# Expert loop of a one-core hybrid SSD/gMLP/MoE step: gate/up of block b, down of block b-1, then the turning of block b's gated rows

## Chip, core and metric

The kernel runs on one core of a Trainium2 chip. The metric is device time in microseconds (us), the median of three runs. All numbers of the profile come from one profiled execution. Engines are PE (matrix multiplication; PEld are its weight loads), DVE (VectorE), ACT (ScalarE), POOL (GpSimd) and SP (the queue of plain transfers). Each engine runs its own instruction stream in program order and meets the others through semaphores. Its sequencer reads that stream; in the rows PEldq, DVEq, ACTq and POOLq are instructions which a sequencer carries out itself.

## What is computed

One step of an encoder layer over 4096 prompt rows and 128 sample rows (33 tiles of 128 rows, 1024 columns, float32): mixing layers first, then a mixture of experts and a last norm. The change touches only the mixture. Each row goes to 2 of 32 experts; its 8448 (row, expert) slots are sorted by expert and padded to blocks of 128 slots:

```
def run_block(args):
    toks, e = args
    xb = h_pad[toks]
    return (jax.nn.silu(xb @ w_gate[e]) * (xb @ w_up[e])) @ w_down[e]
...
ys = ys.reshape(n_slots, -1) * slot_w[:, None].astype(ys.dtype)
out = jnp.zeros((T + 1, ys.shape[1]), ys.dtype).at[slot_tok].add(ys)[:T]
```

`xb` is 128 x 1024, gate and up are 1024 x 256 each, down is 256 x 1024. The number of blocks depends on the data: at least 66, at most 98, and 80 in this execution (block numbers 0 to 79; the count is rounded up to pairs).

## The kernel before

Phase 1 (the mixing layers, 33 tiles) is left as it is. Phase 2 is a loop over expert blocks, unrolled in pairs by `over_pairs`: 33 pairs always run (`SURE`), and each later pair stands in an `If` on a register. Every engine has its own `step(b)`; the order of the calls within it is written by hand and is the order of work.

For block b the chain is: POOL gathers 128 rows (`gather`); ACT copies three quarters of them into other buffers (`move`, 12 copies, L1733) and DVE transposes them in pieces (`turn`, L1778 to L1782) into `hT`; PE multiplies with gate and up (`pe_gate_up`, L1659, 8 matmuls, each float32 matmul two records in the trace); ACT takes the SiLU of the gate half (`silu`, L1741); DVE multiplies it by the up half (`gate`, L1789) and raises `hb_ready`; PE turns the product (`pe_hidden`, L1669); ACT copies it out (`hidden`, L1746) and raises `hbT_out`; PE multiplies with down (`pe_down`, L1678, 4 matmuls) and raises `dn_full`; DVE scales and adds the residual (`weigh`, L1799); POOL stores that as the first result (`keep`, L1560) or the second is added to the first (`earlier`, L1555, and `add_first`, L1807); ACT sums squares (`squares`, L1750), POOL makes the root (`root_of`, L1588 and L1590, raising `fin_r`), DVE applies the last norm (`norm`, L1793, which waits for `fin_r`) and POOL stores (`store`).

POOL's order in `step(b)` is keep(b-1), residual(b+1), gather(b+5), root_of for block b-2, earlier(b), store(b-2). PE's `step(b)` begins with three reads of a table into registers (`pe_weights` and `entry`, L1415: where the weights of a block lie, and how many loads must have landed). Before the change the steps were

```
PE:  gate/up(b+1) k 0..3, hidden(b), gate/up(b+1) k 4..7, down(b)
DVE: weigh(b-1), turn(b+2), gate(b+1), norm, add_first(b-1)
ACT: hidden(b), squares, move(b+3) 0..5, silu(b+1), move(b+3) 6..11
```

and the last PE step also computed a gate/up product of a block that is not there. After the loop DVE, ACT and POOL each read the last block's number from memory into a register (`last_n`, L1833 on DVE); then DVE weighs, adds and norms what is left of the last two blocks, and POOL stores them.

Of the kernel before, what the change touches and what calls it, by code (L numbers as in the profile page):

```python
# [16 lines left out]
I32 = mybir.dt.int32  # L17
# [4 lines left out]
P = 128  # L22
D = 1024
KD = D // P
# [85 lines left out]
def after(eng, sem, n):  # L110

    if n > 0:
        eng.wait_ge(sem, n)
# [8 lines left out]
def build(nc, x_rows, x_cols, consts_in, cols_in, bcast_in, w_in, w_out, w_out_T_in, ws_in, ws_smp_in, cache_in, st_old_in,  # L122
          st_T_in, slot_in, w_exp, final_g, y_out, conv_prompt, ssm_prompt, conv_sample, ssm_sample, gmlp_v_sample):
    ctx = ExitStack()
    with ctx:
# [1281 lines left out]
        y_buf = [x_res[0][:, :], x_res[1][:, :]]  # L1407
        first_i, last_i = (lng_b[:, k * P:(k + 1) * P].bitcast(I32) for k in range(2))
        final_w = mv[:, 0:1]
        final_i = lng_b[:, 2 * P:2 * P + 2].bitcast(I32)  # L1410
        SURE = 2 * T // P // 2
        PAIRS = NBLK // 2
# [129 lines left out]
        def pool_phase2(pool):  # L1542
# [69 lines left out]
            pool.wait_ge(convp_stored, 16)  # L1612
            pool.wait_ge(spill_set, 16)
            residual(0)
            used = over_pairs(pool, step)

            last_n = (pool.value_load(misc[0:1, 4:5], min_val=2 * SURE - 1, max_val=2 * PAIRS - 1), 2 * used)
            for u in range(2):
                pool.wait_ge(s["fin_sq"], last_n[u])
                nc.gpsimd.tensor_tensor(spare[:, u:u + 1], neg_half[:, 0:1], neg_half[:, 0:1], ALU.mult)  # L1620
# [26 lines left out]
        def pe_gate_up(pe, b, weights, k0, k1):  # L1647

            u = b % 2
            slot, loads = weights  # L1650
            if k0 == 0:
                pe.wait_ge(w_loaded, loads)
                if b < 2:
                    for k in range(2):
                        pe.wait_ge(s[f"gx_out{k}"], b + 1)
                after(pe, s["rows_turned"], b - 1)
                after(pe, s["hb_ready"], b - 1)
            for k in range(k0, k1):
                mm = nc.tensor.matmul(PB[u][:, :], hT[u][:, k, :], arena[:, bass.ds(slot + k * 2 * DE, 2 * DE)],  # L1659
                                      start=k == 0, stop=k == KD - 1)  # L1660
            if k1 == KD:
                mm.then_inc(s["gu_full"], 1)

        def pe_hidden(pe, b):

# [5 lines left out]

        def pe_down(pe, b, slot):

            pe.wait_ge(s["hbT_out"], b + 1)
            for n in range(2):
                after(pe, s["dn_out"], 2 * (b - 2) + n + 1)
                for k in range(2):
                    mm = nc.tensor.matmul(dn_bank[b % 2][n], hTb[:, k, :],  # L1678
                                          arena[:, bass.ds(slot + KD * 2 * DE + k * D + n * 512, 512)], start=k == 0, stop=k == 1)
            mm.then_inc(s["dn_full"], 1)  # L1680
# [17 lines left out]
        def pe_phase2(pe):  # L1698
            pe_table_rows(pe)
            pe.wait_ge(s["tables"], 1)  # L1700
            weights0 = pe_weights(pe, 0)
            pe.wait_ge(s["lists_out"], 2)

            def step(b):
                weights = pe_weights(pe, b + 1)
                slot = entry(pe, TAB_SLOT, b, 0, SLOT_AT[2])
                pe_gate_up(pe, b + 1, weights, 0, 4)
                pe_hidden(pe, b)
                pe_gate_up(pe, b + 1, weights, 4, KD)
                pe_down(pe, b, slot)  # L1710
            pe_rows(pe, 0)
            pe_rows(pe, 1)
            pe_gate_up(pe, 0, weights0, 0, KD)
            pe.wait_ge(s["smp_new"], 8)
            over_pairs(pe, step)

        def act_phase2(act):
            act.wait_ge(x2_stored, 16 * NT)
# [31 lines left out]
                nc.scalar.activation(h2[:, :], src, ACT.Square, accum_out=sq[:, u:u + 1]).then_inc(s["fin_sq"], 1)  # L1750

            def step(b):
                hidden(b)
                if b > 1:
                    squares(b % 2, f_buf[b % 2], b - 1)
                move(b + 3, 0, 6)
                silu(b + 1)
                move(b + 3, 6, 12)
            rows0(0)
            rows0(1)  # L1760
            silu(0)
            move(2, 0, 12)
            used = over_pairs(act, step)
            last_n = (act.value_load(misc[0:1, 4:5], min_val=2 * SURE - 1, max_val=2 * PAIRS - 1), 2 * used)
# [4 lines left out]
        def dve_phase2(dve, st):  # L1769
# [37 lines left out]
                V.tensor_tensor(f_buf[u], y_buf[u], m_buf[u], ALU.add).then_inc(s["first_added"], 1)  # L1807

            def step(b):
                if b > 0:  # L1810
                    dve.wait_ge(s["dn_full"], b + 1)
                    dve.wait_ge(x2_back[1 - b % 2], 16 * ((b + 1) // 2))
                    after(dve, first_kept, 16 * (b - 2))
                    weigh(1 - b % 2, wt[:, b - 1:b])
                turn(b + 2)
                gate(b + 1)
                if b % 2 and b // 2 >= SURE - 1:

                    V.tensor_copy(final_i, last_i[:, b - 1:b + 1])
                    V.tensor_copy(final_w, wt[:, b:b + 1])  # L1820
# [6 lines left out]
            dve.wait_ge(s["tables"], 1)  # L1827
            rows1(0)
            rows1(1)
            gate(0)  # L1830
            dve.wait_ge(gf_loaded, 16)
            used = over_pairs(dve, step)
            last_n = (dve.value_load(misc[0:1, 4:5], min_val=2 * SURE - 1, max_val=2 * PAIRS - 1), 2 * used)  # L1833
# [141 lines left out]
```

## Time and profile before

| | us |
|---|---|
| median of 3 runs (lowest, highest) | 2788.34 (2787.91, 2789.7) |
| the profiled execution's own time | 2790.36 |
| its span, first to last instruction | 2788.5 |
| PE busy, share of the span | 2737.2, 98% |
| DVE busy | 1883.0, 68% |
| ACT busy | 1454.7, 52% |
| POOL busy | 818.0, 29% |
| mean granted clock of PE | 0.991 |

The busy times are over the whole span, phase 1 included. In the rows further down a line gives the start (or the stretch), the duration, the engine and line, what is written and read, and in brackets the idle time before and who ended it.

### The profile page before, as it was taken

What the parts mean: (1) busy time and instruction counts of PE and PEld (TensorE: products, weight loads), DVE (VectorE), ACT (ScalarE), POOL (GpSimd) and SP (SyncE); (2) the same over time, 40 slices, a digit from 0 to 9 for tenths busy, and PEclk for the clock granted to TensorE, in tenths of its full rate; (3) what the DMA queues carried; (4) which work ended last, traced back from release to release, by engine and by line L of the source; (5) the groups of instructions that cost most, each with busy time, mean ns of one, the idle gap of its engine ahead of it and who ended that gap; (6) DMA issues with size and microseconds to landing.
All of it is one profiled execution on the core that took longest, in us unless ns stands there. A gap on an engine that the chain in (4) does not pass through costs nothing.

```text
span 2788.5 us, 38529 instructions
## 1 busy us (share of the span) xinstructions
PE 2737.2 (98%) x11715; PEld 1768.6 (63%) x11715; DVE 1883.0 (68%) x5154; ACT 1454.7 (52%) x3396; POOL 818.0 (29%) x1368
## 2 busy tenths in 40 slices
PE   8999999999999999999999999997999999999997
PEld 6777677767776777677767776763444444444443
DVE  5776767676767676767676767665666666666665
ACT  2445544454455444544454445434666666666665
POOL 1121112111211121112111111112556555556555
PEclk9999999999999999999999999998999999999999
DMA  7311111111111111111111111156888677778864
GB/s 305 136 64 46 69 67 48 46 69 61 54 46 69 64 51 46 69 59 56 46 69 61 54 46 61 42 199 252 307 291 294 236 274 255 280 258 293 317 215 146
DMA packets 104914, 377.91 MB, mean 136 GB/s; under 512 B 32713, under 2 KB 34642, under 8 KB 94706
## 3 DMA queue, kind: packets, MB, share of 16 engines
q1 hardware_dynamic: 44226, 236.13, 23.1%
q0 software_dynamic: 60480, 139.24, 14.8%
q8 instruction: 102, 1.67, 0.2%
q14 instruction: 106, 0.87, 0.1%
HBM read 326.14 MB, written 123.03 MB: 161 GB/s over the span
## 4 chain that ended last, share of the span: by engine, by line
PE 95%; DMA 2%; DVE 1%; ACT 1%; issue 1%; SPq 0%; POOL 0%; POOLq 0%; DVEq 0%; ACTq 0%
PE PB L367 24%; PE PB L1659 20%; PE PB L378 16%; PE PB L457 12%; PE SS L1678 5%; PE TB L1678 5%; PE YB L457 4%; PE YB L411 2%; DMA arena<-in_w_in 1%; PE SS L420 1%; PE SS L424 1%; PE TB L433 1%; PE YB L1669 1%; PE MB L402 1%; PE YB L515 0%
## 5 line engine op out<-in xcount | busy, mean ns | idle before, releaser
L367 PE MATMUL PB<-arena,hT 128*128 128x512 f32 (+2 forms) x2112 | 728.3, 498 | 1.8 <-ACT xT L590 1.1
L1659 PE MATMUL PB<-arena,hT 128*128 x1296 | 582.5, 592 | 0.0
L367 PEld LDWEIGHTS PB<-arena,hT 128*128 128x128 f32 x2112 | 396.7, 190 | 276.9 <-issue 229.7
L378 PE MATMUL PB<-hT,arena 128*128 128x128 f32 x4224 | 487.5, 276 | 4.7 <-DVE arena L1148 4.6
L378 PEld LDWEIGHTS PB<-hT,arena 128*128 128x128 f32 x4224 | 481.8, 193 | 8.9 <-issue 4.9
L1659 PEld LDWEIGHTS PB<-arena,hT 128*128 128x128 f32 x1296 | 239.9, 190 | 271.2 <-issue 271.2
L1185 POOL TENSOR_SCALAR rs<-sq 128x2 f32<-128x2 f32 (+1 forms) x66 | 14.2, 216 | 1254.7 <-ACT h L750 910.3
L457 PE MATMUL PB<-arena,tT 128*128 128x274 f32 (+1 forms) x1056 | 361.6, 497 | 0.3 <-ACT tT L644 0.3
L457 PEld LDWEIGHTS PB<-arena,tT 128*128 128x128 f32 x1056 | 197.1, 192 | 142.7 <-issue 123.4
L636 ACT ACTIVATE yb<-ycat 32x128 f32<-32x128 f32 x768 | 235.9, 307 | 89.3 <-DVE ycat L933 48.7
L1789 DVE TENSOR_TENSOR gv<-ycat,PB 128x256 f32<-128x256 f32 x81 | 34.1, 421 | 290.1 <-ACT ycat L1741 280.8
L823 DVE SCALAR_TENSOR_TENSOR xc<-xT,cols,xc 128x128 f32<-128x128 f32 x792 | 216.8, 347 | 3.5
L750 ACT ACTIVATE h<-x_res 128x1024 f32<-128x1024 f32 x33 | 34.9, 1057 | 336.5 <-DVE x_res L942 336.5
L1746 ACT ACTIVATE xdt<-YB 128x256 f32<-128x256 f32 x80 | 30.6, 383 | 280.9 <-PE YB L1669 270.2
L1678 PE MATMUL TB<-arena,xdt 128*128 x320 | 143.9, 592 | 0.0
L1678 PE MATMUL SS<-arena,xdt 128*128 x320 | 143.8, 592 | 0.0
L590 ACT ACTIVATE xT<-PB 128x512 f32<-128x512 f32 x64 | 38.1, 597 | 188.6 <-PE PB L378 187.8
L1733 ACT ACTIVATE zz<-x_in 32x256 f32<-32x256 f32 x320 | 132.0, 413 | 3.8
L457 PE MATMUL YB<-arena,tT 128*128 128x274 f32 x528 | 127.6, 394 | 0.0
L1560 POOL DMA_INDIRECT out_y<-arena,bc x79 | 89.1, 1128 | 95.4 <-DVE arena L1793 84.9
L821 DVE TENSOR_SCALAR xc<-xT,cols 128x128 f32<-128x128 f32 x264 | 70.8, 344 | 66.0 <-issue 66.0
L1555 POOL DMA_INDIRECT xT<-x_rows,bc x81 | 95.6, 1181 | 64.3 <-DMA x_rows<-x_res,bc 34.4
(292 smaller groups left out, 4109.0 us busy)
## 6 DMA issues: line engine op xcount, KB each, us to landing
arena<-in_w_expert SPq DMA_DIRECT2D x32, 2048.0 KB
arena<-in_w_expert SPq DMA_DIRECT2D x32, 1024.0 KB
h_rows<-h SPq DMA_DIRECT2D x34, 512.0 KB, 2.8
x_in<-in_x_rows SPq DMA_DIRECT2D x33, 512.0 KB, 4.4
hT<-in_x_cols SPq DMA_DIRECT2D x33, 512.0 KB, 3.6
x_res<-in_x_rows SPq DMA_DIRECT2D x33, 512.0 KB, 4.2
dec<-running_sums SPq DMA_DIRECT2D x33, 512.0 KB, 3.6
x_rows<-x_res SPq DMA_DIRECT2D x33, 512.0 KB, 2.6
```

Source lines behind the costliest of these rows:

```text
L367: mm = nc.tensor.matmul(out, hT[u][:, k, :], w_group(name)[:, k, :], start=k == 0, stop=k == KD - 1)
L378: mm = nc.tensor.matmul(PB[b][:, c * P:(c + 1) * P], w_block(name, c)[:, k, :], hT[u][:, k, :], start=k == 0, stop=k == KD - 1)
L411: mm = nc.tensor.matmul(bank[:, c], dec[:, h, :], xdt[:, c], start=True, stop=True)
L457: mm = nc.tensor.matmul(out_p[b], tT[:, k, :], w_out_sb[b][:, k, :], start=k == 0, stop=k == KD - 1)
L636: ins = nc.scalar.activation(yb[32 * q:32 * (q + 1), g * P:(g + 1) * P], rows_quarter(b, g, q), ACT.Copy)
L821: ins = V.tensor_scalar(dst, src, tap[:, w, c:c + 1], cols[:, R_CBIAS + c:R_CBIAS + c + 1], ALU.mult, ALU.add)
L823: ins = V.scalar_tensor_tensor(out=dst, in0=src, scalar=tap[:, w, c:c + 1], in1=dst, op0=ALU.mult, op1=ALU.add)
L1555: nc.gpsimd.indirect_dma_start(out=out, out_offset=None, in_=dram, bounds_check=last, oob_is_err=False, in_offset=bass.IndirectOffsetOnAxi ...
L1560: nc.gpsimd.indirect_dma_start(out=dram, in_=src, in_offset=None, bounds_check=last, oob_is_err=False, out_offset=bass.IndirectOffsetOnAxi ...
L1659: mm = nc.tensor.matmul(PB[u][:, :], hT[u][:, k, :], arena[:, bass.ds(slot + k * 2 * DE, 2 * DE)], start=k == 0, stop=k == KD - 1)
L1678: mm = nc.tensor.matmul(dn_bank[b % 2][n], hTb[:, k, :], arena[:, bass.ds(slot + KD * 2 * DE + k * D + n * 512, 512)], start=k == 0, stop= ...
L1733: ins = nc.scalar.activation(moved[g][32 * q:32 * (q + 1), :], quarter(b, g, q), ACT.Copy)
```

## The change

PE's step becomes gate/up(b) whole, down(b-1), hidden(b). DVE's step begins with gate(b), which so stands behind norm and add_first of the step before. ACT's step becomes move(b+2) 0..5, silu(b), move(b+2) 6..11, squares, hidden(b). The loop's last PE step no longer has a gate/up product of a block that does not exist; instead the last down product stands behind the loop and reads its weights' place from `final_slot`, which DVE writes in each pair that may be the last. The reads of the last block's number (`but_one`) move ahead of the loop. POOL's step is as before.

```diff
         def pe_down(pe, b, slot):
-            pe.wait_ge(s["hbT_out"], b + 1)
...
             def step(b):
-                weights = pe_weights(pe, b + 1)
-                slot = entry(pe, TAB_SLOT, b, 0, SLOT_AT[2])
-                pe_gate_up(pe, b + 1, weights, 0, 4)
+                if b == 0:
+                    pe_gate_up(pe, 0, weights0)
+                    pe.wait_ge(s["smp_new"], 8)
+                else:
+                    weights = pe_weights(pe, b)
+                    slot = entry(pe, TAB_SLOT, b - 1, 0, SLOT_AT[2])
+                    pe_gate_up(pe, b, weights)
+                    pe.wait_ge(s["hbT_out"], b)
+                    pe_down(pe, b - 1, slot)
                 pe_hidden(pe, b)
-                pe_gate_up(pe, b + 1, weights, 4, KD)
-                pe_down(pe, b, slot)
             pe_rows(pe, 0)
             pe_rows(pe, 1)
-            pe_gate_up(pe, 0, weights0, 0, KD)
-            pe.wait_ge(s["smp_new"], 8)
-            over_pairs(pe, step)
+            used = over_pairs(pe, step)
+
+            slot = pe.value_load(final_slot, min_val=0, max_val=SLOT_AT[2])
+            pe.wait_ge(s["hbT_out"], 2 * used)
+            pe_down(pe, 2 * SURE - 1, slot)
...
             def step(b):
-                hidden(b)
+                move(b + 2, 0, 6)
+                silu(b)
+                move(b + 2, 6, 12)
                 if b > 1:
                     squares(b % 2, f_buf[b % 2], b - 1)
-                move(b + 3, 0, 6)
-                silu(b + 1)
-                move(b + 3, 6, 12)
+                hidden(b)
             rows0(0)
             rows0(1)
-            silu(0)
-            move(2, 0, 12)
+            but_one = act.value_load(misc[0:1, 4:5], min_val=2 * SURE - 1, max_val=2 * PAIRS - 1)
             used = over_pairs(act, step)
...
             def step(b):
+                if b % 2 and b // 2 >= SURE - 1:
+
+                    V.tensor_copy(final_i, last_i[:, b - 1:b + 1])
+                    V.tensor_copy(final_w, wt[:, b:b + 1])
+                    V.tensor_copy(final_slot, tab[0:1, TAB_SLOT, b:b + 1])
+                gate(b)
                 if b > 0:
                     dve.wait_ge(s["dn_full"], b + 1)
                     dve.wait_ge(x2_back[1 - b % 2], 16 * ((b + 1) // 2))
                     after(dve, first_kept, 16 * (b - 2))
                     weigh(1 - b % 2, wt[:, b - 1:b])
                 turn(b + 2)
-                gate(b + 1)
```

PE in the middle of the loop, before. A step begins with the three table reads (TENSOR_LOAD yb), and the turning L1669 stands between two halves of gate/up; the table reads have the four down matmuls L1678 ahead of them.

```order
L1659 ISA [waits hb_ready,rows_turned,w_loaded]
L1659 MATMUL PB0<-arena,hT0 128x512
...
L1669 MATMUL YB<-cst,gv2 128x128 [waits hbT_out,hb_ready]
L1669 MATMUL YB<-cst,gv2 128x128
L1659 ISA
...
L1678 ISA [waits dn_out,hbT_out]
L1678 MATMUL TB<-arena,xdt 128x512
...
L1415 TENSOR_LOAD yb
L1415 ISA x2
...
L1652 REGISTER_ALU
L1659 ISA [waits hb_ready,rows_turned,w_loaded]
```

The same place now (L1676 is the down product, L1668 the turning, L1416 the table read):

```order
L1676 ISA [waits dn_out,hbT_out]
L1676 MATMUL SS<-arena,xdt 128x512
...
L1668 MATMUL YB<-cst,gv2 128x128 [waits hbT_out,hb_ready]
L1668 MATMUL YB<-cst,gv2 128x128
L1416 TENSOR_LOAD yb
L1416 ISA x2
...
L1652 REGISTER_ALU
L1659 ISA [waits hb_ready,rows_turned,w_loaded]
L1659 MATMUL PB0<-arena,hT0 128x512
```

The turning, with its wait for `hb_ready`, now stands directly ahead of the three table reads and the whole gate/up of the next block.

DVE in the same stretch, before (L1789 is gate, L1793 norm, L1807 add_first, L1799 weigh, L1778 to L1782 turn):

```order
L1799 SCALAR_TENSOR_TENSOR x_res1<-TB,bc 128x512 [waits first_kept,x2_back1,dn_full]
L1799 SCALAR_TENSOR_TENSOR x_res1<-TB,bc 128x512
L1778 STREAM_TRANSPOSE hT0<-zz 128x2x8x32 [waits rows_moved,gu_full]
L1780 STREAM_TRANSPOSE hT0<-xbtok 128x8x32
L1782 STREAM_TRANSPOSE hT0<-xc 32x8x32 x4
L1789 TENSOR_TENSOR gv2<-ycat,PB1 128x256 [waits hbT_full,silu_out]
L1793 SCALAR_TENSOR_TENSOR arena<-arena,rs 128x1024 [waits fin_r]
L1807 TENSOR_TENSOR arena<-x_res1,xT1 128x1024 [waits y_stored1,first_back1,dn_out]
```

And now (L1792 is gate, L1796 norm, L1810 add_first, L1802 weigh):

```order
L1802 SCALAR_TENSOR_TENSOR x_res1<-TB,bc 128x512 [waits first_kept,x2_back1,dn_full]
L1802 SCALAR_TENSOR_TENSOR x_res1<-TB,bc 128x512
L1781 STREAM_TRANSPOSE hT0<-zz 128x2x8x32 [waits rows_moved,gu_full]
L1783 STREAM_TRANSPOSE hT0<-xbtok 128x8x32
L1785 STREAM_TRANSPOSE hT0<-xc 32x8x32 x4
L1796 SCALAR_TENSOR_TENSOR arena<-arena,rs 128x1024 [waits fin_r]
L1810 TENSOR_TENSOR arena<-x_res1,xT1 128x1024 [waits y_stored1,first_back1,dn_out]
L1792 TENSOR_TENSOR gv2<-ycat,PB1 128x256 [waits hbT_full,silu_out]
```

Gate has moved from ahead of norm to behind add_first.

PE at the end of the loop, now: behind the last turning stand the exit and one more register read, and then the last down product.

```order
L1668 MATMUL YB<-cst,gv2 128x128 [waits hbT_out,hb_ready]
L1668 MATMUL YB<-cst,gv2 128x128
L1427 UNCONDITIONAL_BRANCH
L1717 TENSOR_LOAD bc
L1717 ISA x2
L1718 REGISTER_ALU
L1676 ISA [waits dn_out,hbT_out]
L1676 MATMUL TB<-arena,xdt 128x512
```

Before, PE's stream ended with the last down product inside the loop.

## Rows read from the trace of the kernel before

**Rows 1.** Windows: stretch, its length, busy us and count per engine, clock, DMA

```profile
1923.00:2772.00 849.00, 848.76 (x2099) 381.49 (x2096) 540.06 (x893) 546.79 (x1291) 493.26 (x554) 1.00 0.78 271
```

**Rows 2.** Timeline of PE over one period: start, duration, line, count

```profile
2298.17 3.60 PE L1659 MATMUL PB<-arena,hT 128*128 x8
2301.60 0.38 PE L1669 MATMUL YB<-cst,gv 128*128 128x128 f32 x2
2301.82 3.60 PE L1659 MATMUL PB<-arena,hT 128*128 x8
2305.25 3.60 PE L1678 MATMUL TB<-arena,xdt 128*128 x8
2308.69 3.60 PE L1659 MATMUL PB<-arena,hT 128*128 x8
```

**Rows 3.** Timeline of DVE over the same period

```profile
2298.59 1.41 DVE L1799 SCALAR_TENSOR_TENSOR x_res<-SS,bc,xT 128x512 f32<-128x512 f32 x2
...
2300.97 1.79 DVE L1782 STREAM_TRANSPOSE hT<-x_in 32x256 f32<-32x256 f32 x4
2306.44 0.42 DVE L1789 TENSOR_TENSOR gv<-ycat,PB 128x256 f32<-128x256 f32 x1 [3.67 <-ACT ycat L1741]
2306.78 1.28 DVE L1793 SCALAR_TENSOR_TENSOR arena<-arena,rs 128x1024 f32<-128x1024 f32 x1
2307.97 1.22 DVE L1807 TENSOR_TENSOR arena<-x_res,arena 128x1024 f32<-128x1024 f32 x1
2309.11 0.74 DVE L1799 SCALAR_TENSOR_TENSOR x_res<-TB,bc 128x512 f32<-128x512 f32 x1
```

**Rows 4.** Timeline of POOL over the same period

```profile
2300.80 0.99 POOL L1560 DMA_INDIRECT x_rows<-x_res,bc  x1 [1.24 <-DVE x_res L1799]
...
2303.45 1.02 POOL L1555 DMA_INDIRECT x_in<-h_rows,bc  x1 [0.30 <-issue]
...
2304.81 0.56 POOL L1590 TENSOR_TENSOR rs<-rs,cst 128x1 f32<-128x1 f32 x1
```

**Rows 5.** Instructions of L1789 and L1418 at the loop's start: DVE and its sequencer

```profile
1930.55 0.42 DVE L1789 TENSOR_TENSOR gv<-ycat,PB 128x256 f32<-128x256 f32 x1 [6.59 <-ACT ycat L1741]
L1418 DVEq TENSOR_LOAD <-misc x1: 543/543/543, 1930.6 to 1930.6; - x1
1939.70 0.42 DVE L1789 TENSOR_TENSOR gv<-ycat,PB 128x256 f32<-128x256 f32 x1 [1.25 <-ACT ycat L1741]
```

**Rows 6.** PE's sequencer on L1659 behind the turning: ns min/median/max, first and last start

```profile
L1659 PEldq FUSED_REGOPS  x4: 46/46/46, 1931.0 to 1931.4; - x4
L1659 PEldq FUSED_REGOPS  x4: 46/46/46, 1940.2 to 1940.6; - x4
L1659 PEldq FUSED_REGOPS  x4: 46/46/46, 2306.9 to 2307.8; - x4
```

**Rows 7.** PE's sequencer: table reads L1415, and first set-up of L1659 behind them

```profile
L1415 PEldq TENSOR_LOAD <-yb x3: 296/303/305, 2302.9 to 2304.2; - x3
L1659 PEldq FUSED_REGOPS  x4: 46/46/51, 2305.1 to 2305.5; - x4
L1415 PEldq TENSOR_LOAD <-yb x3: 396/907/1137, 2597.5 to 2600.3; - x3
L1415 PEldq TENSOR_LOAD <-yb x3: 901/924/1035, 1925.1 to 1927.7; - x3
```

**Rows 8.** Waits of POOL from 1940 to 2761: total us, times, longest

```profile
POOL x_rows L1560 <- issue: 8.3, 13, 3.6
```

**Rows 9.** Timeline of PE at the loop's start

```profile
1923.07 10.46 PE L1659 MATMUL PB<-arena,hT 128*128 x24
```

**Rows 10.** The loop's end: branches, the register read, and DVE's last weigh

```profile
2757.65 3.60 PE L1678 MATMUL SS<-arena,xdt 128*128 x8
L1428 DVEq COMPARE_BRANCH  x1: 67/67/67, 2770.0 to 2770.0; - x1
L1833 DVEq TENSOR_LOAD <-misc x1: 328/328/328, 2775.1 to 2775.1; - x1
2776.14 1.41 DVE L1799 SCALAR_TENSOR_TENSOR x_res<-TB,mv,bc 128x512 f32<-128x512 f32 x2
```

More of the change, by code:

```diff
@@ L1409, in build @@
         final_w = mv[:, 0:1]
+        final_slot = lng_b[0:1, 2 * P + 2:2 * P + 3].bitcast(I32)
         final_i = lng_b[:, 2 * P:2 * P + 2].bitcast(I32)
@@ L1614, in pool_phase2 @@
             residual(0)
+            but_one = pool.value_load(misc[0:1, 4:5], min_val=2 * SURE - 1, max_val=2 * PAIRS - 1)
             used = over_pairs(pool, step)
-            last_n = (pool.value_load(misc[0:1, 4:5], min_val=2 * SURE - 1, max_val=2 * PAIRS - 1), 2 * used)
+            last_n = (but_one, 2 * used)
             for u in range(2):
@@ L1645, in pe_weights, with pe_gate_up @@
             return entry(pe, TAB_SLOT, b, 0, SLOT_AT[2]), entry(pe, TAB_NTH, b, 1, NE) * 32
-        def pe_gate_up(pe, b, weights, k0, k1):
+        def pe_gate_up(pe, b, weights):
             u = b % 2
             slot, loads = weights
[L1651 to L1658, printed above, removed]
+            pe.wait_ge(w_loaded, loads)
+            if b < 2:
+                for k in range(2):
+                    pe.wait_ge(s[f"gx_out{k}"], b + 1)
+            after(pe, s["rows_turned"], b - 1)
+            after(pe, s["hb_ready"], b - 1)
+            for k in range(KD):
                 mm = nc.tensor.matmul(PB[u][:, :], hT[u][:, k, :], arena[:, bass.ds(slot + k * 2 * DE, 2 * DE)],
                                       start=k == 0, stop=k == KD - 1)
-            if k1 == KD:
-                mm.then_inc(s["gu_full"], 1)
+            mm.then_inc(s["gu_full"], 1)
         def pe_hidden(pe, b):
@@ L1752, in step @@
             def step(b):
-                hidden(b)
+                move(b + 2, 0, 6)
+                silu(b)
+                move(b + 2, 6, 12)
                 if b > 1:
                     squares(b % 2, f_buf[b % 2], b - 1)
-                move(b + 3, 0, 6)
-                silu(b + 1)
-                move(b + 3, 6, 12)
+                hidden(b)
             rows0(0)
             rows0(1)
-            silu(0)
-            move(2, 0, 12)
+            but_one = act.value_load(misc[0:1, 4:5], min_val=2 * SURE - 1, max_val=2 * PAIRS - 1)
             used = over_pairs(act, step)
-            last_n = (act.value_load(misc[0:1, 4:5], min_val=2 * SURE - 1, max_val=2 * PAIRS - 1), 2 * used)
+            last_n = (but_one, 2 * used)
             squares(0, f_buf[0], last_n[0])
@@ L1815, in step @@
                 turn(b + 2)
-                gate(b + 1)
-                if b % 2 and b // 2 >= SURE - 1:
-                    V.tensor_copy(final_i, last_i[:, b - 1:b + 1])
-                    V.tensor_copy(final_w, wt[:, b:b + 1])
                 if b > 1:
@@ L1829, in dve_phase2 @@
             rows1(1)
-            gate(0)
             dve.wait_ge(gf_loaded, 16)
+            but_one = dve.value_load(misc[0:1, 4:5], min_val=2 * SURE - 1, max_val=2 * PAIRS - 1)
             used = over_pairs(dve, step)
-            last_n = (dve.value_load(misc[0:1, 4:5], min_val=2 * SURE - 1, max_val=2 * PAIRS - 1), 2 * used)
+            last_n = (but_one, 2 * used)
             dve.wait_ge(s["first_added"], last_n[0])
```

## The prediction

> **What bounds the kernel now.** The windows view comes first, cut where the expert loop begins and ends. In the loop's 849.00 us PE is busy for 848.76, DVE and ACT for less than two thirds, at a granted clock of 1.00 [rows 1]. So only PE's stream counts here, and what the reader is to see next, in the timeline of one period, is how it is filled. From one gate/up start to the next it takes 2308.69 - 2298.17 = 10.52 us: 16 gate/up records and 8 down records of 3.43/8 = 0.43 us each (6.86 and 3.43), and 0.22 for the turning, with no gap [rows 2]. A faster loop than 10.52 per block is therefore out of reach of any new order; an order can only open gaps. What must be asked is when each thing that PE waits for is ready.
>
> I count from E, the end of a down product, 2298.17 here. DVE, from the same stretch: weigh starts at E + 0.42, the turning of new rows ends at E + 4.59, then DVE idles 3.67 us until SiLU and gate, then norm and add_first follow in 1.19 and 1.14 us, start to start [rows 3]. POOL: keep begins at E + 2.63, and the root that norm needs ends at 2305.37, that is E + 7.20 [rows 4]. Before, that did not matter: norm stood behind gate, which ran at E + 8.27.
>
> **What a wait on PE holds back.** The sequencer view shows it. Gate ends at 1930.97, 1940.12 and 2306.86 [rows 3, 5], and the next register set-up of L1659, which stands behind the turning's wait for `hb_ready`, starts at 1931.0, 1940.2 and 2306.9 [rows 6], each time at once. In those three steps gate ended at quite different points of PE's own work, so this is no chance. DVE does the same: its register read behind the waiting gate starts at 1930.6, when gate starts [rows 5]. I conclude that a waiting instruction holds its sequencer, and that all behind it (table reads too) starts only then. The Trainium skill, "Advanced Engine Details and Errata", section "Sequencer Loop", describes it otherwise: an engine instruction is pushed into the queue and waits there, and others can be read meanwhile. By that rule the table reads would pass the waiting turning; it is one of the rivals below, and these rows speak against it.
>
> **The change, part by part.**
>
> *The steady loop.* Now gate(b+1) stands behind norm and add_first. Norm can start at E + 7.24 (root, and 0.04 as an estimate for the semaphore), add_first 1.19 later, gate 1.14 later at E + 9.57, and it ends 0.42 later at E + 9.99. PE's sequencer, held at the turning, goes on at E + 10.04. Behind the turning stand the three table reads, which once were hidden under the down product: from the first read at 2302.9 to the first set-up of gate/up at 2305.1 it takes 2.16 us in a good step [rows 7]; reads of 0.9 us instead of 0.3 occur (1925.1 and 2597.5), and such a set takes up to 3.8 [rows 7]. I take 2.4 as the middle, as the good case is the common one, and 0.15 for the set-up and the first weight load. Then gate/up and down follow, 10.29 us. So the down product two blocks later ends at E + 10.04 + 2.4 + 0.15 + 10.29 = E + 22.88, where before it ended at E + 21.04: 1.84 us more per two blocks. The chain closes over two blocks because weigh(b-1), which starts it, precedes gate(b+1). The block between adds nothing: it fits in its own 10.5 us.
>
> POOL is sometimes late. In 13 steps keep did not wait for DVE but started late [rows 8], and the root moves with it; those steps were held by transfers still landing. With about 1.2 us for such a step (an estimate: the longest of the 13 waits is 3.6) that is 0.2 us per two-block chain. From 0 to 78 there are 38 such chains of two after the first norm: 38 x (1.84 + 0.2) = 77.5 us. Bounds: reads always good and POOL never late, 38 x 1.60 = 61; reads of 2.7 and 0.35 for POOL, 38 x 2.49 = 95.
>
> If gate were not held by norm, it would end 1.04 us after gate/up's end (first block: 16 of the 24 records end at 1923.07 + 6.87 = 1929.94, gate at 1930.97 [rows 5, 9]). Then 0.05 + 2.4 + 0.15 brings the next gate/up at 3.64 after that end, against 3.43 + 0.24 of down and turning that cover it: no gap, but none to spare. So table reads and norm together make the loss.
>
> *The start.* Gate/up(1) began at 1929.94. Now the turning of block 0 waits for gate(0), 1930.97, then come the reads; those nearest in time took 1925.1 to 1928.9, 3.8 us. Between 2.2 and 3.8 I take 3.0: next gate/up at 1934.2, + 4.2 us (bounds + 3.4 and + 5).
>
> *The end.* The missing gate/up is 6.86 us of PE, but PE did not end the kernel. The last down but one ends at 2757.65 + 3.43 = 2761.08. DVE's sequencer branched out of the loop at 2770.0, its next instruction came at 2775.1, and the last weigh at 2776.14, which is 15.06 after 2761.08 [rows 10]; PE's last down was done at 2771.60. The 5.1 us after the branch are code that is not there yet. (The Trainium skill, "Runtime: NRT & Kernel Launch", section "Instruction fetch mechanics", says that a taken branch out of the fetched window stalls for its page; the trace agrees.) Now the register read after the branch is gone, but the branch still comes after norm is released, at E + 7.4; code at E + 12.5, weigh at E + 12.9: 2.2 us less. PE's own exit, read and last down product, about E + 8 to E + 11, lie ahead of that. The moved table copies and the fewer reads cost nothing: DVE has 3 us idle per step.
>
> *ACT, SP and transfers.* SiLU is ready earlier than before (ACT's first six copies end before gate/up), squares end before POOL's root has its turn, gathers get one block more of time, and weights are released in the old order of gate/up and down. DMA is 0.78 busy [rows 1] and gets more time per block. Nothing here.
>
> Sum: 77.5 + 4.2 - 2.2 = + 79.5 us. The span 2788.5 becomes 2868.0. The profiled execution's own time, 2790.36, lies 2.0 above the median, 2788.34; I put the same difference on the median: 2788.3 + 79.5 = 2868.
>
> **The rivals.**
>
> *The held gate does not hold PE* (the wait sits in the queue, the reads pass it, or norm's root comes early): the turning needs gate at E + 10.0 and PE is there at E + 10.52, so the loop keeps 10.52. By the first form the start costs 1.3 and the end gives 2.2: 2787; with the reads exposed but gate free, + 4.2 - 2.2: 2790. For it: ACT's squares are there early. Against: three of three steps with the sequencer released by gate, and root_of stands behind three transfers on POOL. Chance 0.07, no change.
>
> *Faster*: the removed gate/up comes off in full because the end is PE's, not the code's arrival on DVE. It would take that DVE reaches its last weigh with the last down product, in the loop an unchanged 10.52, and a hidden start: 2788.3 - 6.9 = 2781.5. It decides only if DVE's exit costs under about 1 us in place of 5.1. Chance 0.03.
>
> *The gap comes in every block*: if the chain closed over one block (a late gate delays the weigh that starts the next root), the loss is 78 x about 2 = 156: 2945. In its favour, DVE is one queue; against it, weigh(b) waits for down(b), which ends at E + 10.5 or later, when gate(b+1) is done (E + 9.99). Chance 0.04.
>
> **How the numbers follow.** My forecast, two-block chains of about 23.1 us, has 0.86. Its own range runs from 61 + 3.4 - 2.5 = + 62 to 95 + 5 - 2 = + 98: 2850 to 2886. The remaining 0.14 lies with the rivals on both sides; leaving both out leaves under 2 in 10, and I widen the lower end a little, since POOL may do better in a slower loop: 2846 to 2886. Within 0.2% (5.6 us) is what counts as no change. Faster 0.03, same 0.07, slower 0.90.
>
> **What the changed profile would show.** PE idle in the loop of some 70 to 90 us in place of 0.2; block periods alternating between about 10.5 and 12.4 us, or all near 11.5; DVE's norm waiting for POOL's root in nearly all steps, at 7.2 us after a down product's end; gate at + 9.6 in every step and not at SiLU's end; the table reads starting at gate's end and the first gate/up matmul about 2.5 us behind it. I am wrong if table reads start before gate ends (the hold), if norm starts well before E + 7 (POOL), if the reads take far from 2.4 (size), or if PE's clock falls in the gaps (a cost that I don't charge: all rows above are at 1.00).

## The result and the profile after

| | before | after |
|---|---|---|
| median of 5 runs (lowest, highest), us | 2788.02 (2786.95, 2789.7) | 2866.41 (2862.34, 2867.52) |
| the profiled execution's own time | 2790.36 | 2867.02 |
| its span | 2788.5 | 2865.2 |
| mean granted clock of PE | 0.991 | 0.990 |

The ratio is 1.0278 with a 95% interval from 1.0266 to 1.029. The change makes the kernel 78.4 us slower; 2868 was forecast. (Of all executions in this document one, of the kernel norm_gate_add_root further down, took 6691.75 us; it is not in that kernel's ratio.)

The windows view of after: the stretch that answers to [rows 1], and the loop alone, from the end of down(2) to that of down(78).

```profile
1923.00:2846.00 923.00, 861.41 (x2073) 380.26 (x2072) 544.34 (x897) 540.65 (x1277) 510.54 (x549) 0.99 0.72 247
1965.25:2839.35 874.10, 819.31 (x1977) 361.99 (x1976) 524.00 (x860) 514.49 (x1217) 494.20 (x533) 1.00 0.72 245
```

From the same down product to the same one the loop took 799.58 us before (1961.50 to 2761.08, with no gap) and takes 874.10 now: 74.5 more. The windows view counts PE idle for 874.10 - 819.31 = 54.8 us of the loop (before, 0.2 in the whole stretch); the other 19.7 us it counts as busy. They are products that last longer: the first matmul after a gap is spaced 0.10 us wider, some products run at a lower clock, and the last matmul before a gap is drawn 0.16 us longer than one that another follows. How a gap comes about is seen in the timeline of PE, beside [rows 2]:

```profile
2217.47 3.60 PE L1676 MATMUL SS<-arena,xdt 128*128 x8
2220.90 0.38 PE L1668 MATMUL YB<-cst,gv 128*128 128x128 f32 x2
2222.45 7.13 PE L1659 MATMUL PB<-arena,hT 128*128 x16 [1.17 <-issue]
2229.41 3.60 PE L1676 MATMUL TB<-arena,xdt 128*128 x8
2232.84 0.38 PE L1668 MATMUL YB<-cst,gv 128*128 128x128 f32 x2
2233.06 7.04 PE L1659 MATMUL PB<-arena,hT 128*128 x16
2239.93 3.60 PE L1676 MATMUL SS<-arena,xdt 128*128 x8
```

In the timeline of DVE, beside [rows 3] (L1796 is norm, L1810 add_first, L1792 gate, L1802 weigh):

```profile
2227.91 1.28 DVE L1796 SCALAR_TENSOR_TENSOR arena<-arena,rs 128x1024 f32<-128x1024 f32 x1 [2.63 <-POOL rs L1591]
2229.11 1.22 DVE L1810 TENSOR_TENSOR arena<-x_res,arena 128x1024 f32<-128x1024 f32 x1
2230.25 0.42 DVE L1792 TENSOR_TENSOR gv<-ycat,PB 128x256 f32<-128x256 f32 x1
2233.05 1.41 DVE L1802 SCALAR_TENSOR_TENSOR x_res<-TB,bc 128x512 f32<-128x512 f32 x2 [2.38 <-PE TB L1676]
```

And PE's sequencer reading its table behind the gate that ended at 2219.72 + 0.42 = 2220.14:

```profile
L1416 PEldq TENSOR_LOAD <-yb x3: 296/296/297, 2220.2 to 2221.5; - x3
```

Read together: down(24) ends at E = 2220.90. Norm waits for the root and starts at E + 7.01, add_first at E + 8.21, gate at E + 9.35 and ends at E + 9.77. The three reads begin at once when a gate has ended, although PE itself is still in the down product and turns only at 2220.90: it is the semaphore that releases the sequencer, not the matmul. The first gate/up product comes 2.31 us (at 2222.45) or 2.39 us (at 2233.06) behind the end of its gate. Two blocks on, E(26) is 2243.37, 22.47 us after E(24).

The loss of a pair can also be spread over both of its blocks: E(44), E(45) and E(46) are 2450.21, 2461.72 and 2472.77, periods of 11.51 and 11.05 with 22.56 in sum. So 55 blocks of the loop have a gap over 0.05 us ahead of gate/up, though the chain closes over two.

The waits from 1940 to 2840 (engine, what waits, for whom: us in total, times, longest):

```profile
DVE arena L1796 <- POOL rs L1591: 208.5, 77, 5.0
PE PB L1659 <- issue: 50.8, 53, 2.0
DVE gv L1792 <- ACT ycat L1745: 15.1, 7, 6.6
DVE arena L1810 <- DMA out_y<-arena,bc: 12.8, 12, 2.3
```

Norm waited for the root 77 times. Gate waited for SiLU only 7 times; before, that was where DVE idled. "issue" on L1659 is PE without a wait that the profile shows: the register reads. The last row shown, add_first waiting for a store, is the one that had no place in the forecast.

The loop's end, answering to [rows 10]: PE's last turning and last down product, its sequencer's exit branch, DVE's branch, then DVE.

```profile
L1429 PEldq COMPARE_BRANCH  x8: 80/80/3803, 2678.5 to 2838.8; - x8
L1429 DVEq COMPARE_BRANCH  x8: 43/43/67, 2687.7 to 2848.1; - x8
```

```profile
2839.35 0.38 PE L1668 MATMUL YB<-cst,gv 128*128 128x128 f32 x2
2843.63 5.39 PE L1676 MATMUL TB<-arena,xdt 128*128 x8 [3.90 <-issue]
...
2847.93 1.29 DVE L1796 SCALAR_TENSOR_TENSOR arena<-arena,rs 128x1024 f32<-128x1024 f32 x1 [4.20 <-POOL rs L1591]
...
2852.47 0.06 DVE L1839 MEMSET spare<- 128x1 f32 x1 [2.12 <-issue]
...
2852.80 1.41 DVE L1802 SCALAR_TENSOR_TENSOR x_res<-TB,mv,bc 128x512 f32<-128x512 f32 x2
```

DVE branches at 2848.1 and its next instruction comes at 2852.47; the last weigh stands at 2852.80, 13.45 after E(78) = 2839.35. From E(78) the kernel needs 25.85 us to its end, before 27.42.

### The profile page after: what moved, and what is told of

Read it like the earlier page. It is cut to its first block, busy times and chain, and to the rows that moved or that the text cites. A ratio compares the mean times of both kernels' runs of the same rounds, so it can differ in the third digit from the quotient of the medians.

```text
span 2865.2 us, 38474 instructions
## 1 busy us (share of the span) xinstructions
PE 2752.9 (96%) x11699; PEld 1768.2 (62%) x11699; DVE 1889.9 (66%) x5161; ACT 1449.3 (51%) x3383; POOL 840.4 (29%) x1368
## 4 chain that ended last, share of the span: by engine, by line
PE 90%; DMA 3%; issue 3%; DVE 1%; POOL 1%; ACT 1%; SPq 0%; POOLq 0%; DVEq 0%; ACTq 0%
PE PB L367 24%; PE PB L1659 18%; PE PB L378 16%; PE PB L457 12%; PE SS L1676 4%; PE TB L1676 4%; PE YB L457 4%; PE YB L411 2%; DMA out_y<-arena,bc 1%; DMA arena<-in_w_in 1%; PE SS L420 1%; PE SS L424 1%; PE TB L433 1%; PE YB L1668 1%; PE MB L402 1%
## 5 line engine op out<-in xcount | busy, mean ns | idle before, releaser
L1659 PE MATMUL PB<-arena,hT 128*128 x1280 | 573.7, 601 | 53.9 <-issue 52.7
L1659 PEld LDWEIGHTS PB<-arena,hT 128*128 128x128 f32 x1280 | 238.4, 191 | 338.9 <-issue 338.6
L1796 DVE SCALAR_TENSOR_TENSOR arena<-arena,rs 128x1024 f32<-128x1024 f32 x79 | 101.5, 1285 | 212.7 <-POOL rs L1591 212.7
L1745 ACT ACTIVATE ycat<-PB 128x256 f32<-128x256 f32 x80 | 30.7, 383 | 241.9 <-PE PB L1659 241.9
L1676 PE MATMUL TB<-arena,xdt 128*128 x320 | 145.7, 598 | 3.9 <-issue 3.9
L1561 POOL DMA_INDIRECT x_rows<-x_res,bc x79 | 78.3, 991 | 227.6 <-DVE x_res L1802 219.7
L1676 PE MATMUL SS<-arena,xdt 128*128 x320 | 143.9, 592 | 0.0
L1556 POOL DMA_INDIRECT xT<-x_rows,bc x81 | 108.7, 1341 | 67.4 <-DMA x_rows<-x_res,bc 32.5
```

What stands on the lines that cost most here:

```text
L1556: nc.gpsimd.indirect_dma_start(out=out, out_offset=None, in_=dram, bounds_check=last, oob_is_err=False, in_offset=bass.IndirectOffsetOnAxi ...
L1561: nc.gpsimd.indirect_dma_start(out=dram, in_=src, in_offset=None, bounds_check=last, oob_is_err=False, out_offset=bass.IndirectOffsetOnAxi ...
L1676: mm = nc.tensor.matmul(dn_bank[b % 2][n], hTb[:, k, :], arena[:, bass.ds(slot + KD * 2 * DE + k * D + n * 512, 512)], start=k == 0, stop= ...
L1796: V.scalar_tensor_tensor(out=rows, in0=rows, scalar=rs[:, u:u + 1], in1=gf_b, op0=ALU.mult, op1=ALU.mult).then_inc(s["fin_out"], 1)
```

## The experiments

The theory: two things together make the loss. PE's order puts three register reads and a whole gate/up behind the turning's wait for the gate, and DVE's order puts the gate behind what norm waits for. The rivals: one of the two alone does it, or the hold of the sequencer has no part in it. The loop column is the time from the end of down(2) to that of down(78) in each profile; before it was 799.58. Ratios are to the kernel before, run beside it. The profiled execution is not always near the median: it was the slowest of four in root_early (2856.87) and the quickest of four in reads_ahead (2799.87) and in add_gate_norm (2836.11).

| kernel | PE's order | DVE's order behind turn | loop | median | ratio, 95% |
|---|---|---|---|---|---|
| pe_only | new | gate, norm, add | 799.60 | 2792.12 | 1.0014 (1.0005 to 1.0024) |
| dve_only | old | norm, add, gate | 799.58 | 2788.43 | 1.0000 (0.999 to 1.0009) |
| pe_dve | new | norm, add, gate | 873.23 | 2868.86 | 1.0291 (1.0274 to 1.0309) |
| norm_gate_add | new | norm, gate, add | 820.98 | 2814.21 | 1.0096 (1.0079 to 1.0113) |
| add_gate_norm | new | add, gate, norm | 840.96 | 2839.61 | 1.0184 (1.0167 to 1.0201) |
| norm_gate_add_root | new | norm, gate, add; root early | 799.71 | 2791.73 | 1.0009 (0.9999 to 1.0019) |
| root_early | new | norm, add, gate; root early | 864.08 | 2851.73 | 1.0225 (1.021 to 1.0241) |
| reads_ahead | new, reads before the turning | norm, add, gate | 810.61 | 2804.73 | 1.006 (1.0043 to 1.0077) |
| reads_twice | new, six reads | norm, add, gate | 964.91 | 2961.02 | 1.0617 (1.06 to 1.0633) |
| mid_turn | turning amid gate/up | norm, add, gate | 799.58 | 2787.54 | 0.9998 (0.9989 to 1.0007) |
| mid_turn_root | turning amid gate/up | norm, add, gate; root early | 799.58 | 2786.68 | 0.9994 (0.9984 to 1.0003) |

**Each order alone, and both.** In the kernel before, PE alone is changed (hidden(b), reads, gate/up(b+1) whole, down(b)), then DVE alone, then both:

```diff
 (pe_only, in PE's step)
+                pe_hidden(pe, b)
                 weights = pe_weights(pe, b + 1)
                 slot = entry(pe, TAB_SLOT, b, 0, SLOT_AT[2])
-                pe_gate_up(pe, b + 1, weights, 0, 4)
-                pe_hidden(pe, b)
-                pe_gate_up(pe, b + 1, weights, 4, KD)
+                pe_gate_up(pe, b + 1, weights, 0, KD)
                 pe_down(pe, b, slot)
 (dve_only, in DVE's step)
                 turn(b + 2)
-                gate(b + 1)
...
                     add_first(b - 1)
+                gate(b + 1)
```

> The kernel before with PE's order alone changed: turning of block b ahead of the table reads and of the whole gate/up(b+1). DVE and ACT as before, and the gate/up product of the block that is not there stays. Theory (the loss is gate held behind norm, in series with the table reads behind the held turning): gate is on time here, about 1.0 us after gate/up's end, so PE idles only where a table read is slow, 0 to 0.3 us per block; with about 3.8 us at the start that gives 2792 to 2803 us. Rival (the new order on PE alone costs the loss, whatever DVE does): about 2866.

> The kernel before with DVE's order alone changed: gate(b+1) behind norm and add_first. Theory: gate ends about 9.8 us after a down product's end, and PE needs it only after half of the next gate/up, 13.9 us after it, so nothing is lost: 2787 to 2791 us. Rival (DVE's order alone is the loss): about 2860.

> Both of these edits in the kernel before, nothing else of the change. Theory: the loss is there only with both, in series: about 74 us in the loop and 3.8 at the start, no gain at the end: 2864 to 2870 us. Rival (something else of the change makes the loss, ACT's order or the reads moved ahead of the loop): clearly under 2840.

pe_only measured 2792.12, dve_only 2788.43, pe_dve 2868.86, all as expected. In pe_only's DVE and PE timelines the gate again waits for SiLU and the loop has no gap:

```profile
2317.05 0.42 DVE L1788 TENSOR_TENSOR gv<-ycat,PB 128x256 f32<-128x256 f32 x1 [3.33 <-ACT ycat L1740]
```

```profile
2309.56 7.03 PE L1659 MATMUL PB<-arena,hT 128*128 x16
2316.43 3.60 PE L1678 MATMUL SS<-arena,xdt 128*128 x8
2319.86 0.38 PE L1669 MATMUL YB<-cst,gv 128*128 128x128 f32 x2
```

The gate ends at 2317.47, 2.39 before PE is done with the down product at 2319.86 and 2.61 before the next gate/up could start: the reads just fit. So the loss is neither part's; it needs both. ACT's new order, the exit and the missing product, which pe_dve leaves as they were, change little: pe_dve is within 3 us of the changed kernel.

**The reads.** In the changed kernel, the reads for the next block are put ahead of the turning; and in another, they are done twice:

```diff
 (reads_ahead, in PE's step)
+                    weights, slot = ahead["next"]
                     pe_gate_up(pe, b, weights)
                     pe.wait_ge(s["hbT_out"], b)
                     pe_down(pe, b - 1, slot)
+                ahead["next"] = (pe_weights(pe, b + 1), entry(pe, TAB_SLOT, b, 0, SLOT_AT[2]))
                 pe_hidden(pe, b)
 (reads_twice)
+                    pe_weights(pe, b)
+                    entry(pe, TAB_SLOT, b - 1, 0, SLOT_AT[2])
                     weights = pe_weights(pe, b)
                     slot = entry(pe, TAB_SLOT, b - 1, 0, SLOT_AT[2])
```

> The changed kernel with the three table reads for the next block moved ahead of the turning, so that they don't stand behind its wait. Gate stays behind norm. Theory: gate at 9.8 us after a down product's end is in time for the turning at 10.5, and nothing but the set-up of a matmul follows it, so the loop is back at 10.5 us per block; the start costs 1 us, the end gives 1.6: 2785 to 2792 us. Rival (gate behind norm costs PE time by itself): over 2820.

> The changed kernel with the three table reads done twice in each PE step (the first set's values aren't used). Theory: the reads stand in the chain that closes over two blocks, once per chain, so one more set (about 1.95 us) adds 38 x 1.95 = 74 us: 2930 to 2950 us, and the pair of block periods grows from 22.5 to about 24.4 us. Rival (PE's gaps come in every block and each pays for its own reads): twice that, about 3015. Rival (reads overlap with waiting, they are no cost): 2866.

reads_ahead measured 2804.73, which gives back 61.7 of the 78.4 us, but is 13 us above the range that I expected. Its DVE timeline shows the remainder:

```profile
2256.69 1.28 DVE L1798 SCALAR_TENSOR_TENSOR arena<-arena,rs 128x1024 f32<-128x1024 f32 x1 [2.64 <-POOL rs L1591]
2259.12 1.23 DVE L1812 TENSOR_TENSOR arena<-x_res,xT 128x1024 f32<-128x1024 f32 x1 [1.14 <-DMA out_y<-arena,bc]
```

Norm is on time, but add_first waits 1.14 us for a store, and the gate behind it comes too late for the turning. The turning was late 13 times in the loop, by 8.4 us in sum, after a late addition as here or after a late root (at the down product of block 21 it came as late as in the changed kernel). That lateness had no place in my expectation.

reads_twice measured 2961.02, 94.6 us above the changed kernel and 11 us above my range; the loop alone has 964.91 - 874.10 = 90.8 more, 2.39 us for each of 38 two-block chains. The rival of one more set per block, 3015, is out. The timelines separate the parts, over the 38 pairs from block 2 to block 78: from the gate's end to the first product it takes 4.44 us in the mean in place of 2.41, so the second set itself costs 2.03 us a chain, 77.2 in all, near the 1.95 that I took. Gates that come later add 7.2, and longer products 6.4. The longer products are mostly those at a lower clock: PE's granted clock fell eight times in this loop, twice in that of the changed kernel, and once in the stretch below (PE's timeline), where gate/up took 8.82 us in place of 7.13. PE's sequencer reads six values ahead of that product, where it read three:

```profile
L1416 PEldq TENSOR_LOAD <-yb x6: 299/302/317, 2226.7 to 2229.9; - x6
```

```profile
2230.86 8.82 PE L1659 MATMUL PB<-arena,hT 128*128 x16 [3.69 <-issue]
...
2245.04 7.13 PE L1659 MATMUL PB<-arena,hT 128*128 x16 [1.70 <-issue]
```

**The root early.** In the changed kernel, POOL makes the root right behind keep, ahead of the issue of two gathers:

```diff
+                if b > 1:
+                    pool.wait_ge(s["fin_sq"], b - 1)
+                    root_of(b % 2, b - 1)
                 residual(b + 1)
                 gather(b + AHEAD)
-                if b > 1:
-                    pool.wait_ge(s["fin_sq"], b - 1)
-                    root_of(b % 2, b - 1)
```

> The changed kernel with one edit on POOL: root_of stands right behind keep, ahead of residual and gather, so that norm need not wait for it. PE, DVE and ACT as in the changed kernel. Theory: root ends 4.6 us after a down product's end in place of 7.0, gate is on time (about 1 us after gate/up's end), PE idles only for slow table reads: 2788 to 2800 us. Rival (norm and add_first ahead of gate are too long by themselves, whatever POOL does): over 2830.

It measured 2851.73 instead of 2788 to 2800: my theory fell. The root is early (E + 4.3) as meant, yet the waits of DVE in the loop (1945 to 2838) now read

```profile
DVE arena L1810 <- DMA out_y<-arena,bc: 94.1, 39, 7.1
...
DVE arena L1796 <- POOL rs L1591: 3.2, 4, 2.3
```

The 208 us of waiting for the root are gone, and add_first waits 94.1 us in 39 steps for the store whose buffer it writes. A place in the two timelines, three rows of DVE and then the store's issue on POOL:

```profile
2312.47 1.35 DVE L1796 SCALAR_TENSOR_TENSOR arena<-arena,rs 128x1024 f32<-128x1024 f32 x1
2317.30 1.23 DVE L1810 TENSOR_TENSOR arena<-x_res,arena 128x1024 f32<-128x1024 f32 x1 [3.48 <-DMA out_y<-arena,bc]
2318.44 0.41 DVE L1792 TENSOR_TENSOR gv<-ycat,PB 128x256 f32<-128x256 f32 x1
```

```profile
2306.88 1.01 POOL L1561 DMA_INDIRECT out_y<-arena,bc  x1 [0.30 <-issue]
```

The store was issued at 2306.88 and the addition could start at 2317.30, 10.4 us later. The rival's number, over 2830, came true but not its reason: where no store was waited for (behind E(10), say, at 2059.66), the gate started at E + 7.70, waiting for SiLU, and PE had no gap. So the gate stands behind two waits, norm's for the root and add_first's for a store, and the first hides the second. The early root did not make the stores slower: the median from a store's issue to its landing was 5.6 us here, 5.8 in reads_ahead, where the root is late, and 6.2 with and 6.0 without the early root in the last two kernels below. It is the addition that came earlier.

**One wait at a time.** With PE's new order, DVE's gate goes between norm and add_first (with the root late and early), or between add_first and norm:

```diff
 (norm_gate_add; norm_gate_add_root moves the root as above besides)
                 if b > 1:
                     norm(b % 2, f_buf[b % 2], b - 1)
+                gate(b + 1)
                 if b > 0:
                     add_first(b - 1)
 (add_gate_norm)
                 if b > 0:
                     add_first(b - 1)
+                gate(b + 1)
                 if b > 1:
                     norm(b % 2, f_buf[b % 2], b - 1)
```

In add_gate_norm ACT also has a wait for its own earlier squares, long fulfilled when it comes to it.

> The kernel before with TensorE's new order (as in pe_only), and on VectorE the gate of block b+1 between the normalisation and the addition: one wait (for the root, over GpSimd) ahead of the gate, and the wait for the transfers behind it. E is the end of a down product. Theory (the gate stands behind two waits, and each has its own price): the normalisation ends at E+7.0, the gate at about E+8.3 in every second block, and with 2.4 us to the first gate/up product and 10.29 us of products the pair takes 21.0 to 21.3 us instead of 21.04: 0 to 10 us in 38 pairs, and about 4 us at the start as in pe_only. Time 2791 to 2804 us. Rival (the root's wait alone is enough, the addition and its transfers add little): 2835 us or more.

> As norm_gate_add, with the root on GpSimd ahead of the residual's and the gather's issue (as in root_early). Theory: the gate has left the addition's wait behind it and the root is at E+4.3, so the gate ends before E+6.5 and TensorE has no gap in the loop: 2788 to 2797 us. Rival (the early root makes the transfers late, and these hold VectorE through the next step as well, wherever the gate stands): 2810 us or more, with the gates late by what an addition waited one step before.

> As norm_gate_add, but the addition ahead of the gate and the normalisation behind it: one wait ahead of the gate, that for the transfers (store of three blocks before, first choice's row, residual). Theory: the store that the addition waits for is issued behind a normalisation that now stands last, so it is later while the addition comes sooner (about E+5.5 instead of E+7.1), and some additions wait for it. Gates at about E+7.8 where the transfers are there and up to 5 us later where not; time between 2796 and 2840 us, nearest to 2810. Rival (transfers land in time whatever the order, what root_early showed came from the root's place alone): 2791 to 2796 us, as pe_only.

norm_gate_add measured 2814.21, 10 us above the range of the theory and 21 below the rival. The DVE timeline shows the chain as expected:

```profile
2232.17 1.28 DVE L1792 SCALAR_TENSOR_TENSOR arena<-arena,rs 128x1024 f32<-128x1024 f32 x1 [2.63 <-POOL rs L1590]
2233.38 0.41 DVE L1788 TENSOR_TENSOR gv<-ycat,PB 128x256 f32<-128x256 f32 x1
```

The down product before it ended at 2225.16, so the gate ends at E + 8.63, and a pair of blocks takes 21.3 to 21.4 us in place of 21.04. That makes 38 x 0.30 = 11; the loop has 21.4 more. Of the other 10 us, late gates make 8 and longer products 2.5. The gate was late where the root was (E + 8.7 at the down product of block 14, E + 9.3 at that of block 21), and the steps behind it too, as there is nothing left to absorb it. At block 14 transfers stood behind both engines (one row of POOL's timeline, one of DVE's): POOL had waited 4.90 us for the landing of the kept block, and DVE's addition 2.25 us for a store.

```profile
2093.94 1.18 POOL L1555 DMA_INDIRECT arena<-x_rows,bc  x1 [4.90 <-DMA x_rows<-x_res,bc]
2092.95 1.23 DVE L1806 TENSOR_TENSOR arena<-x_res,xT 128x1024 f32<-128x1024 f32 x1 [2.25 <-DMA out_y<-arena,bc]
```

norm_gate_add_root has no gap in the loop (799.71) and 2791.73 us: this expectation held, though add_first still waited for stores:

```profile
DVE arena L1806 <- DMA out_y<-arena,bc: 33.2, 26, 3.0
DVE arena L1792 <- POOL rs L1590: 10.4, 18, 2.3
```

Now these 33.2 us stand behind the gate and cost nothing. add_gate_norm measured 2839.61, at the upper end of my range: the early addition waits most of all.

```profile
DVE arena L1807 <- DMA out_y<-arena,bc: 149.8, 52, 6.9
```

So each wait makes a loss of its own when it alone stands ahead of the gate: 21.4 us in the loop for the root's (with some lateness from transfers in it, as said), 41.4 for the store's where the addition comes first. With norm's wait ahead of it the addition comes later and mostly finds its store landed (12.8 us of waiting in the changed kernel). The changed kernel, with both, loses 74.5; 38 x 1.14 = 43 us of that, as an estimate, is the addition's own duration, which then stands between the root's wait and the gate.

**The turning back in its place.** The changed kernel with the turning of block b-1 between the halves of gate/up(b), the last turning behind the loop, and still no gate/up of a block that does not exist; and the same with the early root:

```diff
-                    pe_gate_up(pe, b, weights)
+                    pe_gate_up(pe, b, weights, 0, 4)
+                    pe_hidden(pe, b - 1)
+                    pe_gate_up(pe, b, weights, 4, KD)
                     pe.wait_ge(s["hbT_out"], b)
                     pe_down(pe, b - 1, slot)
-                pe_hidden(pe, b)
```

> The changed kernel with the turning of block b-1 back between the halves of gate/up(b), and the last turning behind the loop. The missing gate/up product, DVE's order (gate behind norm) and ACT's stay as changed. Theory: gate at 9.8 us after a down product's end is early for a turning at 13.9, and the table reads have the down product for cover, so the loop is 10.52 us per block with no gap, the start costs nothing, the end gives up to 2 us: 2785 to 2789 us. Rival (the missing gate/up product comes off in full once PE has no gaps): 2781 to 2782.

> mid_turn and root_early together. Theory: the end of the kernel is set by DVE, whose sequencer branches out of the loop only when the last norm in the loop is released; with the root 2.4 us earlier its code comes 2 us earlier or more, so 3 to 6 us less than before: 2782 to 2786 us. Rival (the end is set by PE's last down product or by POOL's transfers): as mid_turn, 2785 to 2789.

2787.54 and 2786.68: no gap in the loop with either. This also measures the missing gate/up by itself. PE is done with its last down product 4.83 us after E(78) instead of 10.52, but DVE branches at 2767.8 and goes on at 2771.96 whatever PE does (timelines of PE, then of DVE's last weigh):

```profile
2760.36 3.70 PE L1678 MATMUL TB<-arena,xdt 128*128 x8 [0.91 <-ACT xdt L1755]
```

```profile
2772.29 1.41 DVE L1807 SCALAR_TENSOR_TENSOR x_res<-TB,mv,bc 128x512 f32<-128x512 f32 x2
```

From E(78) to the end it is 25.6 us (24.6 with the early root) in place of 27.4. mid_turn_root lies just above its expected 2782 to 2786: the early root shortened the end by 1.0 us and not by the 2 or more that I took. Neither kernel can be told from the one before by its time (0.9998 and 0.9994, both intervals include 1), so no version here beats it by what the runs can show.

## Why the prediction was right

The median, 2866.41, lies 1.6 below the forecast, and the mechanism is the one that was forecast. That the number came so close is luck in part: two terms were off by 15.6 and 12.6 us and nearly cancelled. The two profiled executions differ by 76.7 us (2865.2 - 2788.5), where 79.5 was forecast, and the medians by 1.7 more than that. By the steps:

- **PE's stream is all that counts before.** Right: the loops that keep the gate's reads covered (pe_only, mid_turn, norm_gate_add_root) all take 799.6 to 799.7 us.
- **The held gate holds the reads.** Right. reads_ahead, which only takes the reads out from behind the wait, gives back 61.7 us. The Trainium skill's "Sequencer Loop" in "Advanced Engine Details and Errata", by which the reads could have passed the waiting turning, is not borne out by this trace: the reads of after start within 0.1 us of the gate's end.
- **The chain closes over two blocks.** Right: 22.47 us per pair in the undisturbed steps, and reads_twice adds 2.39 per pair, not per block. The rival whose chain closes over one block, with 2945 us, is out; that 55 blocks have a gap is the loss of a pair spread over both of its blocks.
- **The chain's length**, 22.88 forecast. The undisturbed chain is 0.41 shorter. The root comes at E + 6.98 and not E + 7.20, since weigh now starts with the down product's end and keep with it; that brings the gate's end to E + 9.77 (forecast 9.99). Reads and set-up take 2.41 in the mean, not 2.60. So 38 x 1.43 = 54.3 us are the undisturbed chain (forecast 69.9).
- **The allowance for lateness**, 0.2 per pair, was too small, and this is the step of the forecast that was wrong in kind too. Over the 38 pairs from block 2 to block 78, gates later than E + 9.77 add 17.4 us (0.46 a pair), 12 of the 38 gates being late by more than 0.1 us. Two of the 12 gates, behind down(16) and down(22), were 3.8 late each, and hold a fall of the clock told below. I had put it all on POOL, and under transfers had written "Nothing here" (that transfers held POOL in its 13 late steps stood there too, but rows 8 name none). In fact add_first waited 12 times for a store, up to 2.3 us; the late roots are the other part. Another 2.8 us come from products that take 10.37 rather than 10.29 when PE starts them from idle. 54.3 + 17.4 + 0.1 (reads) + 2.8 = 74.6, against 74.5 measured and 77.5 forecast: 15.6 too much for the undisturbed chain, 12.6 too little for all the rest.
- **The start**, + 4.2 forecast, + 3.75 measured (E(0) from 1940.46 to 1944.21), by other terms. Gate/up(0) ended 1.3 us earlier in this execution; from its end to E(0) it took 15.57 us, where it took 10.52 before. The reads came in the good form, 0.30 each, and the first product 2.36 behind the gate; but then the clock fell, and gate/up(1) took 8.82 us instead of 7.13 (PE's timeline):

```profile
1929.83 0.41 PE L1668 MATMUL YB<-cst,gv 128*128 128x128 f32 x2 [1.02 <-DVE gv L1792]
1932.11 8.82 PE L1659 MATMUL PB<-arena,hT 128*128 x16 [1.88 <-issue]
```

- **The end**, - 2.2 forecast, - 1.57 measured. The mechanism was right (the saved register read, not the missing product): weigh stands at E(78) + 13.45 and not + 12.9, because norm was released at E + 8.58, 1.2 later than I took, so the branch came later.
- **PE's idle time**, forecast as 70 to 90 us. The windows view, the one from which the 0.2 before was read, shows 54.8 in the loop and 61.6 in the stretch from 1923 to 2846; the rest of the loss is counted as busy time.
- **The clock**, not charged. It fell to 0.50 for 3.4 us twice in the loop, after gaps, once at the start and once in the last down product. The sum above holds them: a late gate behind down(15) shows how.

For the changed kernel: the timeline of PE (two rows), of DVE (one), and the windows around the fall, in which the third number from the end is PE's clock:

```profile
2124.54 0.44 PE L1668 MATMUL YB<-cst,gv 128*128 128x128 f32 x2 [1.47 <-DVE gv L1792]
2126.79 8.83 PE L1659 MATMUL PB<-arena,hT 128*128 x16 [1.81 <-issue]
```

```profile
2122.93 1.22 DVE L1810 TENSOR_TENSOR arena<-x_res,xT 128x1024 f32<-128x1024 f32 x1 [2.25 <-DMA out_y<-arena,bc]
```

```profile
2120.00:2127.10 7.10, 3.81 (x11) 1.54 (x10) 4.81 (x8) 4.21 (x11) 2.73 (x3) 1.00 0.73 258
2127.10:2130.50 3.40, 3.40 (x5) 1.33 (x4) 1.43 (x4) 2.23 (x6) 2.72 (x4) 0.50 0.69 200
```

A store that had not landed made the addition 2.25 us late, the gate and the turning with it, PE stood idle for 3.3 us around the turning, and the next product ran for 3.4 us at the lower of the clock's two levels: 1.7 us more. Block 17 has a period of 15.98 us for this reason. Block 23 has 15.99, with a fall of the clock too, but there it was the root that came late, at E + 9.32.

The rival "norm's root comes early, so the loop keeps 10.52" would have been wrong even with its condition met: root_early made the root early and lost 63 us all the same.

## What to carry to other kernels

Ahead of an instruction whose wait holds a sequencer, put everything that needs no wait: register reads and address arithmetic above all. On the engine that feeds such a wait, keep the short product that the other engine waits for ahead of work that waits for third parties. Before moving it behind such work, count every wait ahead of it, not only the one that ends last in the profile: that one hides the others, and taking it away uncovers them. A mended order is cheap to test with one wait ahead at a time.

## What the runs showed of the hardware

- A tensor instruction that waits for a semaphore holds the register reads behind it; they go on within 0.1 us of the semaphore, before the instruction itself has run (reads from 2220.2, turning at 2220.90). A set of three reads with its arithmetic costs 2.3 to 2.4 us where nothing covers it; a second set made that 2.03 us longer in the mean (reads_twice).
- A taken branch out of the loop: PE's sequencer spent 3.80 us in it, and DVE's next instruction stood 4.4 us behind its own. The Trainium skill states such a stall ("Runtime: NRT & Kernel Launch", "Instruction fetch mechanics"); the trace agrees as far as it goes, since it shows the time and not what was fetched.
- PE's granted clock fell to 0.50 (1.2 GHz) for 3.4 us beside idle times of PE like those shown (1.47 + 1.81 and 1.02 + 1.88 us in after, 3.69 in reads_twice), but not beside most: twice in the loop of after, which has 55 gaps ahead of gate/up, and eight times each in the loops of reads_twice and root_early. What tells the gaps that are followed by a fall from the rest was not tried.
- A store of 128 rows issued by POOL could hold its buffer for 10.4 us, where the median from issue to landing was 5.6 (root_early). Whether it waits in its queue behind the gathers issued just ahead of it, or for the memory, stays open: no run changed the queue or its load.
